# A first attention that goes head by head, with its value products in column tiles

## What is computed

```
def masked_softmax(s, mask):
    s = jnp.where(mask, s.astype(jnp.float32), -jnp.inf)
    m = jnp.max(s, axis=-1, keepdims=True)
    ...
    p = jnp.exp(s - m)
    return p / jnp.maximum(jnp.sum(p, axis=-1, keepdims=True), 1e-30)

# token heads: for each query the 128 best keys of the indexer, and only those up to its position
s = jnp.einsum('bthd,btkd->bthk', qi, k_sel) * HEAD_DIM ** -0.5
p = masked_softmax(s, valid[:, :, None, :]).astype(v.dtype)
return jnp.einsum('bthk,btkd->bthd', p, v_sel)
...
# memory heads
s = jnp.einsum('bshd,bnhd->bhsn', q, k).astype(jnp.float32) * HEAD_DIM ** -0.5
p = jax.nn.softmax(s, axis=-1).astype(v.dtype)
return jnp.einsum('bhsn,bnhd->bshd', p, v).reshape(B, S, MEM_Q)
```

## Time and profile before

| | |
|---|---|
| runs | 2463.72, 2469.21, 2471.77 us |
| median | 2469.21 us |
| span of the profiled execution | 2468.0 us |
| TensorE (PE) busy | 2423.7 us, 98% |
| weight loads (PEld) | 2004.0 us, 81% |
| VectorE (DVE) / ScalarE (ACT) / GpSimd (POOL) | 936.0 / 1079.6 / 972.3 us |
| mean granted clock of TensorE | 0.996 |

### The profile page before, as it was taken

How to read it: one execution, slowest core, us unless ns; L and a number is a source line. 1 busy time by engine, 2 the same in 40 slices (tenths; PEclk the granted TensorE clock), 3 DMA queues, 4 the chain that set the end, 5 groups by cost and what they waited for, 6 DMA issues and landing times.

```text
span 2468.0 us, 36248 instructions
## 1 busy us (share of the span) xinstructions
PE 2423.7 (98%) x11990; PEld 2004.0 (81%) x11990; DVE 936.0 (38%) x2051; ACT 1079.6 (44%) x1917; POOL 972.3 (39%) x484
## 2 busy tenths in 40 slices
PE   8999999999999999999999999999999999999998
PEld 6888888888778978888887978788888797788886
DVE  7976322211477753222214243321211773311212
ACT  7565443432347754444335534432332583432321
POOL 4821444444331124444443413444443423444441
PEclk9999999999999999999999999999999999999999
DMA  4300333333420013233332312233333202233331
GB/s 154 116 30 18 90 97 101 94 102 105 128 69 10 1 35 94 93 102 93 103 102 79 103 39 81 77 95 95 100 94 94 69 18 69 86 101 95 94 94 68
DMA packets 57866, 202.75 MB, mean 82 GB/s; under 512 B 7072, under 2 KB 7968, under 8 KB 57392
## 3 DMA queue, kind: packets, MB, share of 16 engines
q1 hardware_dynamic: 54864, 196.02, 26.2%
q10 hardware_dynamic: 2912, 5.55, 0.6%
HBM read 199.44 MB, written 2.10 MB: 82 GB/s over the span
## 4 chain that ended last, share of the span: by engine, by line
PE 41%; issue 14%; POOL 7%; ACT 1%; DVE 1%; POOLq 0%; DVEq 0%; ACTq 0%
PE bank L764 36%; POOL w_lo L618 7%; PE bank L1008 1%; PE bank L967 1%; PE bank L979 1%; ACT h_hi L1492 1%; PE bank L1372 0%; PE bank L1353 0%; ACT gained L1495 0%; PE bank L1367 0%; PE bank L793 0%; PE bank L1055 0%; PE bank L881 0%; PE bank L770 0%; PE bank L786 0%
## 5 line engine op out<-in xcount | busy, mean ns | idle before, releaser
L618 POOL TENSOR_TENSOR w_lo<-w_raw,w_hi 128x1024 fp32r<-128x1024 f32 x368 | 883.3, 2401 | 1197.7 <-ACT w_hi L1449 1188.1
L764 PE MATMUL bank<-h_hi,w_hi 128*128 128x512 f32 x1648 | 650.5, 395 | 7.2 <-DVE tmp L2476 2.1
L764 PE MATMUL bank<-h_lo,w_hi 128*128 128x512 f32 x1648 | 642.2, 390 | 0.0
L764 PE MATMUL bank<-h_hi,w_lo 128*128 128x512 f32 x1648 | 642.2, 390 | 0.0
L1449 ACT ACTIVATE w_hi<-w_raw 128x1024 fp32r<-128x1024 f32 x368 | 386.8, 1051 | 242.7 <-PE bank L764 214.0
L764 PEld LDWEIGHTS bank<-h_hi,w_hi 128*128 128x128 f32 x1648 | 309.8, 188 | 82.3 <-issue 5.9
L764 PEld LDWEIGHTS bank<-h_hi,w_lo 128*128 128x128 f32 x1648 | 309.7, 188 | 65.2
L764 PEld LDWEIGHTS bank<-h_lo,w_hi 128*128 128x128 f32 x1648 | 309.9, 188 | 65.0 <-issue 2.2
L764 PE MATMUL bank<-mact_hi,w_hi 128*128 128x512 f32 x512 | 199.3, 389 | 1.7 <-DVEq L2342 1.7
L764 PE MATMUL bank<-mact_hi,w_lo 128*128 128x512 f32 x512 | 199.2, 389 | 0.0
L764 PE MATMUL bank<-mact_lo,w_hi 128*128 128x512 f32 x512 | 199.2, 389 | 0.0
(11 more groups left out here) (403 smaller groups left out, 3489.3 us busy)
## 6 DMA issues: line engine op xcount, KB each, us to landing
w_raw<-in_weights SPq DMA_DIRECT2D x368, 512.0 KB, 3.6
out<-x ACTq DMA_DIRECT2D x8, 256.0 KB, 2.1
x<-in_xT SPq DMA_DIRECT2D x4, 256.0 KB, 6.8
x<-in_xT ACTq DMA_DIRECT2D x4, 256.0 KB, 7.4
memx<-in_memT SPq DMA_DIRECT2D x1, 1024.0 KB, 9.8
cmp_w1k<-in_cmp_w ACTq DMA_DIRECT2D x1, 1024.0 KB, 5.6
cmp_w1v<-in_cmp_w ACTq DMA_DIRECT2D x1, 1024.0 KB, 7.5
rope_c<-in_rope_c SPq DMA_DIRECT2D x1, 256.0 KB, 8.4
```

The lines of the kernel that those rows point to most:

```text
L618: nc.gpsimd.tensor_tensor(w_lo[:, t % RING, :], w_raw[:, t % RAW, :], w_hi[:, t % RING, :].bitcast(F32), ALU.subtract).then_inc(lo_ready, 1)
L764: r = nc.tensor.matmul(out, a, b, start=first and n == 0, stop=last and n == 2)
```

## The change

- **By heads.** "dsa" and "mem0" leave `attention_stream`. `attention_by_heads` has an order of its own, without a loop: TensorE does the values of the four units of head h, the transposes of units 0 and 1 of head h + 1, the four scores of head h + 2, and the transposes of units 2 and 3 of head h + 1. ScalarE moves unit 1, exponentiates unit 0 of the next head, moves units 2 and 3 and exponentiates the other three. VectorE moves unit 0, takes four maxima, and writes the output of a whole head.
- **Buffers.** The weights of a head and their transposes have tiles of their own, `prob_heads` and `probT_heads`, each for two heads of up to ten key tiles. The waits that keep a buffer from being overwritten look two heads back.
- **Column tiles.** The value product of a key tile is two products: one with the first 64 of its 128 query columns as stationary operand, one with the other 64. Their outputs are partitions 0 to 63 and 64 to 127 of one bank, and the four units of a head lie side by side in it.
- **Sums.** `dsa_v` and `v_mem` have a 65th column of ones, so column 64 of the output is the sum of the weights. The exponentials have no accumulator any more, and VectorE does one reciprocal of four columns and one product for a head.

The other two attentions keep `attention_stream` and `pair_of_heads`.

```diff
+HEADS0 = UNIT0["nsa0"] // TT
...
+def head_units(head):
+    if head >= HEADS0:
+        return []
+    kind, n = ("dsa", head) if TT * head < UNIT0["mem0"] else ("mem0", head - UNIT0["mem0"] // TT)
+    pair, i = (0, n // 2) if kind == "dsa" else (n // 2, 0)
+    return [(kind, pair, TT * (n % 2) + qt, i) for qt in range(TT)]
...
 def moved_by_vector(kind, u):
-    return not kind.startswith(("nsa", "swa")) and u % 4 == 1
+    return kind == "mem1" and u % 4 == 1
...
-            dsa_v = sb("dsa_v", [P, TT, HD], where=s)
+            dsa_v = sb("dsa_v", [P, TT, HD + 1], where=s)
+            w_uv = sb("w_uv", [P, HD], where=s)
...
+                prob_heads = sb("prob_heads", [P, 2, 10 * P], where=s2)
+                probT_heads = sb("probT_heads", [P, 2, 10 * P], where=s2)
...
-        v_mem = sb("v_mem", [P, DEPTH, 2, 2 * P])
+        v_mem = sb("v_mem", [P, DEPTH, 2, 4, HD + 1])
...
+        def head_sums(g):
+            return o_bank[g // TT % 2][:, 0:TT * (HD + 1)].rearrange("p (a n) -> p a n", a=TT)
...
             def values(kind, pair, u, i):
...
                 pe.wait_ge(probT_ready[g % 2], g // 2 + 2 + per // 2 * i)
-                if not kind.startswith("swa"):
+                if in_heads(kind):
+                    if u % TT == 0 and g + per * i >= 2 * TT:
+                        pe.wait_ge(o_done, g - 2 + per * i)
+                elif not kind.startswith("swa"):
...
-                    r = nc.tensor.matmul(output_place(kind, u, g), probT[:, g % 2, n * P:(n + 1) * P], v, start=n == 0, stop=n == len(kts) - 1)
+                    halves = (slice(0, HD), slice(HD, P)) if in_heads(kind) else (slice(0, P),)
+                    for rows in halves:
+                        w = p[:, n * P + rows.start:n * P + rows.stop]
+                        r = nc.tensor.matmul(output_place(kind, u, g)[rows, :], w, v, start=n == 0, stop=n == len(kts) - 1)
...
+            def transposes_then_scores(transposed_head, scored_head):
+                turned, scored = head_units(transposed_head), head_units(scored_head)
+                for unit in turned[0:2]:
+                    transposes(*unit)
+                for unit in scored:
+                    scores(*unit)
+                for unit in turned[2:4]:
+                    transposes(*unit)
+
+            def attention_by_heads(banks_free):
...
+                transposes_then_scores(0, 1)
+                for head in range(HEADS0):
+                    for unit in head_units(head):
+                        values(*unit)
+                    transposes_then_scores(head + 1, head + 2)
...
-            attention_stream(pe, STREAMS[0], lambda at: attention_begin(at, banks_free), pair_of_heads)
+            attention_by_heads(banks_free)
...
+                if in_heads(kind):
+                    nc.scalar.activation(p, score_bank[bank_of(kind, u)][:, 0:p.shape[1]], ACT.Exp, bias=nmax[:, s4:s4 + 1],
+                                         scale=1.0 if kind.startswith("mem") else -1.0).then_inc(probs_ready, 1)
+                    return
...
+            def moves_and_exponentials(moved_head, weighed_head):
+                moved, weighed = head_units(moved_head), head_units(weighed_head)
+                for unit in moved[1:2]:
+                    move_transposed(*unit)
+                for unit in weighed[0:1]:
+                    exponentials(*unit)
+                for unit in moved[2:4]:
+                    move_transposed(*unit)
+                for unit in weighed[1:4]:
+                    exponentials(*unit)
...
+                if in_heads(kind):
+                    if u % TT == TT - 1:
+                        four, sums = slice(s4 - TT + 1, s4 + 1), head_sums(g)
+                        dve.wait_ge(pv_done, g + 3 + per * i)
+                        nc.vector.reciprocal(rinv[:, four], sums[:, :, HD]).then_inc(rinv_ready, 1)
+                        dve.wait_ge(rinv_ready, (g + per * i) // TT + 1)
+                        nc.vector.tensor_tensor(o_tok[:, :, of_head], sums[:, :, 0:HD],
+                                                rinv[:, four].rearrange("p (a b) -> p a b", b=1).to_broadcast([P, TT, HD]),
+                                                ALU.mult).then_inc(o_done, TT)
+                    return
...
+            nc.vector.memset(dsa_v[:, :, HD:HD + 1], 1.0)
```

More of the change, by code:

```diff
@@ L186, in look_ahead, with in_heads, prob_columns @@
     return 5 if kind.startswith("swa") else 4
+def in_heads(kind):
+    return kind in ("dsa", "mem0")
+def head_units(head):
[4 more added lines that the diff above has]
+    return [(kind, pair, TT * (n % 2) + qt, i) for qt in range(TT)]
+def prob_columns(kind, u):
+    qt, n = u % TT, P * len(key_tiles(kind, u % TT, 1))
+    start = P * (qt * (qt + 1) // 2) if kind == "dsa" else n * qt
+    return slice(start, start + n)
 def moved_by_vector(kind, u):
-    return not kind.startswith(("nsa", "swa")) and u % 4 == 1
+    return kind == "mem1" and u % 4 == 1
 def bank_of(kind, u):
@@ L1616, in pair_of_heads, with attention_by_heads @@
                     unit_of_pair(u, at)
+            def moves_and_exponentials(moved_head, weighed_head):
[8 more added lines that the diff above has]
+                    exponentials(*unit)
+            def attention_by_heads():
+                for unit in head_units(0):
+                    exponentials(*unit)
+                for head in range(HEADS0):
+                    moves_and_exponentials(head, head + 1)
             def concat(prefix, n):
@@ L2289, in pair_of_heads, with move_then_maxima, attention_by_heads @@
                     unit_of_pair(u, at)
+            def move_then_maxima(moved_head, scored_head):
+                for unit in head_units(moved_head)[0:1]:
+                    move_transposed(*unit)
+                for unit in head_units(scored_head):
+                    maximum(*unit)
+            def attention_by_heads():
+                for unit in head_units(0):
+                    maximum(*unit)
+                move_then_maxima(0, 1)
+                for head in range(HEADS0):
+                    move_then_maxima(head + 1, head + 2)
+                    for unit in head_units(head):
+                        output(*unit)
             def concat(prefix, n):
@@ L2378, in _ @@
             nc.vector.memset(eps[:, :], EPS).then_inc(consts_made, 1)
+            nc.vector.memset(dsa_v[:, :, HD:HD + 1], 1.0)
+            for l in range(DEPTH):
+                nc.vector.memset(v_mem[:, l, :, :, HD:HD + 1].rearrange("p a h n -> p (a h) n"), 1.0)
             zero_sum("attn0")
```

59 lines of the change are left out of this document (44 added, 15 removed).

## The result

| | us |
|---|---|
| after, 4 runs | 2448.39 to 2453.70, median **2450.91** |
| before, 4 runs beside them | 2463.72 to 2471.77, median 2467.57 |
| ratio | 0.9934, interval 0.9919 to 0.9948 |
| profiled execution of after: own time / span | 2453.70 / 2451.9 |

The kernel is faster by 16.7 us, where 12 were forecast. Of the 6 us, 4.7 are gain that was not forecast. The rest is the starting point, since the kernel before took 2467.57 us beside the change and the forecast set out from 2469.21. In a later series on another occasion the same kernel took 2448.70 us (2448.10 to 2450.06) against 2466.27 before, ratio 0.9925 [0.9908, 0.9941].

The account below looks back on a forecast made before the run. TensorE's queue was taken as the bound, busy 98% of the span. "dsa" heads 7.9 us, memory heads 5.0, end -1: net 12; 2468.0 - 12 + 1 gives 2457 us, range 2452 to 2470.

Parts of the forecast that it names:

- The halves run side by side: Value products of the first attention: both 64-column tiles work together, some 0.06 us per pass of both, 0.12 per key tile.
- halves in turn: Rival for the value products: the two tiles are not active together, 0.21 us per key tile, 2469 us; chance 0.20.
- a price per pass: Rival for the value products: issuing each pass costs 0.104 us, 0.42 per key tile, 2501 us, slower; chance 0.10.
- The sign that the prediction named: In the changed profile, two value passes start within 0.01 us of each other on weight tiles of 128*64.
- the 1.2 to 1.3 named as a sign: Values of a "dsa" head in the changed profile: its 40 passes take 1.2 to 1.3 us.
- I charge 0.15 per head for this and for a late second exponential: Values right behind a head's last two transposes: TensorE waits for ScalarE's last move, 0.15 us per head (0 to 0.4).
- Gain 0.16 per head, nothing to 0.3: Writing out the loops ends TensorE's wait at the loop edge in every second head: 0.16 us per head.
- the values and scores of a "dsa" head: Values in column tiles, 1.5 us instead of 2.0, gain 0.5; scores of four units together, gain 0.15 per head.
- its 0.3 for the change of shape: Around a head's values the array changes its shape and back: 0.3 us for in and out.
- memory head: Values, scores and transposes of a memory head together take 4.3 us against 5.56, 5.0 us gained for 4.
- begin and end of the stage: At the end, no scores cover the last head's moves and one larger product precedes the concat: -1 us.
- 2 us less: Behind the stage TensorE's clock falls to 0.50; without that fall the time would be 2 us less.

Follow-up runs that it names:

- the unrolled kernel: The kernel before with the hardware loop over the "dsa" heads written out, nothing else: 2464.44 us, ratio to before 0.9988.
- its repetition: The changed kernel, unaltered, measured once more on a later occasion: 2448.70 us (2448.10 to 2450.06), against 2466.27 for the kernel before.
- Pairs without quarters: The changed kernel with the units of two memory heads taken in turns, values still in two column tiles: 2448.01 us, ratio to before 0.9916.
- the version with all three: The changed kernel with memory heads' units in turns, values in four 32-column tiles, and a second tile for the queries: 2445.34 us, ratio to before 0.9911.
- scores first: The changed kernel with a head's four scores ahead of all four transposes instead of between the second and third: 2455.85 us (one run).
- halves apart: The changed kernel with all first halves of a unit's key tiles ahead of all its second halves: 2452.73 us (one run).

## Why the prediction was right and wrong

**What held.** TensorE's queue was the bound and what it lost came off the end. The halves run side by side, as the index products of the earlier trace rows had it: 0.058 us per pair of half passes where 0.06 was expected. The two rivals that would have taken the gain away fell: halves in turn need 0.21 per key tile, a price per pass more, and it is 0.12. The sign that the prediction named is there: the starts in the records of after, in us, for the first head above come in pairs 0.007 us apart, and the pairs follow each other by 0.058 to 0.061.

```
154.680 154.687   154.739 154.745   154.797 154.804   154.855 154.862   154.916 154.923
```

The first pair (154.573 and 154.580) stands 0.107 ahead of the next, which is part of what entering the shape costs. The head's forty passes take 1.38 and not the 1.2 to 1.3 named as a sign; a part of the cost of the shape and the short wait for the move are in them.

**What failed.** The mechanism was right and the sizes of terms in the sum were off. The step that failed first is "I charge 0.15 per head for this and for a late second exponential". The wait exists, but it is 0.05 per head: the values start right behind the seven transposes (154.57 in the row above), the first three units cover 0.76 us, and the fourth finds its move just ended (155.27, first pass 155.330). The charge took 1.2 us too much from the gain. The second is "Gain 0.16 per head, nothing to 0.3" for the loop, sized by the one visible edge; a head of the unrolled kernel gives 0.25, 1.1 us more over twelve. The third is the values and scores of a "dsa" head, 0.65 forecast and 0.75 measured. Against the unrolled kernel the values take 1.33 without that wait instead of 1.91, the scores 1.36 instead of 1.56, and the transposes 1.15 instead of 1.12, because they carry the entry into the shape: 0.58 + 0.20 - 0.03. The forecast had 0.5 and 0.15; its 2.0 us at full width were 0.09 too many, and its 0.3 for the change of shape is 0.24. Term by term, per head and in all:

| | forecast | measured | difference in all |
|---|---|---|---|
| wait for the last move | -0.15 | -0.05 | 12 x 0.10 = 1.2 |
| loop | 0.16 | 0.25 | 1.1 |
| values and scores of "dsa" | 0.65 | 0.75 | 1.2 |
| memory head | 5.56 - 4.3 = 1.26 | 1.38 | 4 x 0.12 = 0.5 |
| begin and end of the stage | -1 | -1.0 | 0 |

That is 4.0 of the 4.7 us. The other 0.7 has no term of its own; the clock alone moves more than that from execution to execution. Nor would these errors have left the range by themselves: 2469.21 - 16.7 is 2452.5, just inside. The lower time of the kernel before, 2467.57, took the result the last 1.6 us out of it.

**The clock.** The prediction took this term as zero, "2 us less" without the fall behind the stage. The fall was indeed absent, and another stood 130 us earlier. The windows of the whole program show more of them, in after at 93 to 100, 600 to 650, 1400 to 1450 and 1900 to 1950 us, in its repetition only the first. The profiled execution of the kernel before has them too, behind the stage, at 1400 to 1450, at 1950 to 2000 (0.93, a fall of twice the length) and at 2000 to 2050 us. One such window, first of after, then of its repetition:

```profile
1400.00:1450.00 50.00, 47.65 (x232) 36.80 (x231) 19.45 (x37) 17.67 (x34) 10.69 (x5) 0.97 0.16 53
```

```profile
1400.00:1450.00 50.00, 47.73 (x238) 37.08 (x238) 19.47 (x38) 17.67 (x34) 9.56 (x4) 1.00 0.17 55
```

Three falls fewer, and the span is 2451.9 - 2447.0 = 4.9 us shorter with the same program: 1.6 us each, which is 50 x 0.03 = 1.5 by the windows. Pairs without quarters had four falls in its profiled execution (span 2449.1), the version with all three one (2442.9); of the 6.2 us between them 4.9 are falls and 1.3 is the edit, near the 1.0 expected. So much of what a median of four runs shows below 5 us is how often the clock fell. The gain of the change is not: in the later series five runs of the kernel before and three of the change have a mean granted clock of 0.999, and their medians are 2464.94 and 2448.57 us, 16.4 apart.

Does the early fall belong to the change? The repetition of the change had it at the same place, which its expectation gave as the sign that it does (95 to 100 us at 0.66). But the kernel before with column tiles alone has it as well (0.66), while scores first, halves apart and the version with all three run those microseconds at 1.00. It is in seven of the ten profiled executions in the new order and in one of the three in the old one. So it is tied to neither; whether the new order makes it more frequent stays open.

**A rule against the trace.** In the row of after forty loads of 64 weight columns and their products, all on the same 128 rows, take 1.38 us; one load in turn with one product would have been the rival's 2.1. The Trainium skill, "TensorE: Matmul & The Clock Gate", section "The mechanism" in Part 3, lets a weight load overlap products in flight only where the row groups differ. The trace disagrees with that sentence for column tiles. The same section also lets a load go ahead that targets the background weight buffer; no run here shows whether the loads of the halves do that. The Trainium skill, "TensorEngine Tiling (Array Packing)", says under "Key Properties" that tiles operate independently, load and product in parallel, and that a change of mode drains the engine. The trace agrees with the first: a pair of half passes comes every 0.058 us, where a pass at full width takes 0.112, 1.9 times the rate. It fits the second in that a visit costs 0.24 us; that a drain is what costs it is not shown. The Trainium skill, "TensorE: Matmul & The Clock Gate", section "Wait — 56ns, not 53.3ns?", gives 62 ns per product with the hardware decoder off. No run shows how the decoder was set; the trace shows only that this price is not paid here: the starts of two half passes stand 0.007 us apart, and eighty quarter passes take 1.35 us, 0.017 each.

## What to carry to other kernels

Cutting a weight tile in columns pays where a pass takes longer than its stream (0.112 us for 65 columns here, 0.058 in two tiles); each visit to the tiled shape costs about 0.24 us here, so gather the small products into one visit before cutting them (0 us gained in the old order, 10 in the new). Put independent work of the right length between the pieces of a chain that share two banks: the same instructions with the scores at another place were 5 to 10 us slower. Read such waits from start to start, since a bracket of 0.26 stood for 0.45 to 0.50, and 0.05 in every head had no bracket at all. And before a difference of a few microseconds is given a cause, count the clock falls in the windows of both profiles.

## What the runs showed of the hardware

- Passes of 65 fp32 columns in different column tiles start 0.007 us apart, and each tile takes one about every 0.058 us, with two tiles or with four.
- A pass of 64 or of 65 fp32 columns at full width costs 0.112 us inside a row of passes; in column tiles both cost the same too. The first pass of a row at full width takes only 0.057 to 0.059, and the last one ahead of the scores 0.08.
- Entering column tiles costs 0.09 to 0.10 us in the transposes ahead. Another 0.14 comes once per visit, of which 0.05 stands behind the first pair of passes.
- The other half's passes may stand four passes away at almost no cost (1.13 against 1.09 for 32), while units with up to eight lose 0.28 per head.
- A pause of 2.5 us at 92 us came with a lower clock in 8 of 13 profiled executions and with none in the other 5; each fall cost 1.6 us.
